# A second attention layer and the choice of experts, per token tile between the slots of one gather

## The reference

```
for i in (0, 1):
    h = x * scale + shift                                   # from c, per layer and half
    f = short_conv_mixer(h) if i == 0 else diff_attention(h)
    x = layer_norm(a * x + gate * f)
    h = x * scale + shift
    x = layer_norm(a * x + gate * peer_ffn(h))

diff_attention: q, k, v = split(h @ w_qkv)                  # 8 heads, 2 scores each, causal
    p = softmax(q k^T / 8 - slope * distance);  a = p[0] - lam * p[1]
    out = rms_norm(a v) * (1 - lambda_init) @ w_o
peer_ffn: q = h @ w_q                                       # 8 heads x 2 x 128
    s = q . sub_keys (2 x 128 scores a head); top 16 of each half; top 16 of the 256 sums
    out = sum over 8 x 16 experts of softmax(top) * gelu(h . u[idx]) * v[idx]
```

## Time and profile before

| | |
|---|---|
| time, median of 3 runs | 2627.26 us (2626.95, 2627.26, 2642.89) |
| the profiled execution | 2643.78 us, span 2641.8 us, mean granted TensorE clock 0.925 |
| busy: PE, PEld, DVE, ACT, POOL | 2226.3, 1465.6, 1677.9, 1113.8, 649.1 us |
| gather, `arena<-experts` | 512 indirect DMAs; its queue moved 587.24 MB |
| weights, `wring<-w_stream` | 284 DMAs of 512 KB |
| chain that ended last | PE 46%, DMA 34%, DVE 10%, ACT 5% of the span |

### The profile page before, as it was taken

One profiled execution on the slowest core, in us unless ns is written; L12 is line 12 of the kernel. 1 busy time (PEld: TensorE's weight loads), 2 busy tenths in 40 slices (PEclk: granted clock), 3 DMA queues, 4 the chain that ended last, 5 costly groups with the idle time before them and its releaser, 6 DMA issues.

```text
span 2641.8 us, 30239 instructions
## 1 busy us (share of the span) xinstructions
PE 2226.3 (84%) x10668; PEld 1465.6 (55%) x10668; DVE 1677.9 (64%) x3715; ACT 1113.8 (42%) x2737; POOL 649.1 (25%) x636
## 2 busy tenths in 40 slices
PE   7678999999999998887787877789688887787786
PEld 7546999876999997522222222277683222222222
DVE  4774667554676666577676666456665766666655
ACT  4343543532453433444444444345344444444443
POOL 0000000000001003444444444300054444344341
PEclk8768999985899988999999999987899999999999
DMA  5223577532557644899999999933258999999995
GB/s 202 78 88 125 172 246 246 184 136 80 179 187 286 236 150 152 315 421 422 421 421 421 421 422 419 401 92 105 66 207 353 421 422 421 422 421 421 422 421 220
DMA packets 130924, 742.66 MB, mean 281 GB/s; under 512 B 14432, under 2 KB 16224, under 8 KB 64992
## 3 DMA queue, kind: packets, MB, share of 16 engines
q0 software_dynamic: 87552, 587.24, 54.5%
q1 hardware_dynamic: 42512, 152.12, 17.5%
q10 hardware_dynamic: 720, 1.51, 0.2%
HBM read 739.76 MB, written 1.05 MB: 280 GB/s over the span
## 4 chain that ended last, share of the span: by engine, by line
PE 46%; DMA 34%; DVE 10%; ACT 5%; issue 3%; POOL 2%; SPq 0%; DVEq 0%; POOLq 0%; ACTq 0%
DMA arena<-experts,arena 34%; PE bank L471 10%; PE bank L473 10%; PE bank L472 10%; PE bank L830 7%; DVE arena L1831 3%; PE bank L586 2%; POOL arena L437 1%; ACT arena L1243 1%; PE bank L573 1%; PE bank L615 1%; ACT arena L1242 1%; PE bank L552 1%; ACT whi L1003 1%; POOL wlo L424 1%
## 5 line engine op out<-in xcount | busy, mean ns | idle before, releaser
L830 PE MATMUL bank<-arena 128*128 128x512 f32 x2048 | 1015.3, 628 | 265.2 <-ACT arena L1243 265.1
L1831 DVE CUSTOM_DVE_ANT_0 arena<-arena 128x1024 f32<-128x1024 f32 x512 | 627.0, 1225 | 444.9 <-DMA arena<-experts,arena 444.7
L830 PEld LDWEIGHTS bank<-arena 128*128 128x128 f32 x2048 | 364.2, 194 | 909.5 <-ACT arena L1243 609.1
L437 POOL DMA_INDIRECT arena<-experts,arena x512 | 541.0, 1057 | 757.5 <-PE bank L830 704.9
L471 PE MATMUL bank<-hTh,whi 128*128 128x256 f32 (+1 forms) x1472 | 439.2, 298 | 52.7 <-DVE hTl L1412 42.6
L1403 DVE TENSOR_TENSOR wlo<-wring,whi 128x1024 fp32r<-128x1024 f32 x260 | 316.4, 1224 | 244.5 <-ACT whi L1003 243.8
L472 PE MATMUL bank<-hTl,whi 128*128 128x256 f32 (+1 forms) x1472 | 430.5, 292 | 0.0
L473 PE MATMUL bank<-hTh,wlo 128*128 128x256 f32 (+1 forms) x1472 | 430.1, 292 | 0.0
L1003 ACT CAST whi<-wring 128x1024 fp32r<-128x1024 f32 x284 | 295.9, 1047 | 239.7 <-PE bank L473 238.3
L1239 ACT ACTIVATE arena<-arena 128x1 f32<-128x1 f32 x512 | 103.6, 202 | 673.4 <-DVE arena L1831 672.5
L471 PEld LDWEIGHTS bank<-hTh,whi 128*128 128x128 f32 x1472 | 291.3, 198 | 66.7 <-issue 51.3
(11 more groups left out here) (253 smaller groups left out, 2473.2 us busy)
## 6 DMA issues: line engine op xcount, KB each, us to landing
wring<-w_stream SPq DMA_DIRECT2D x284, 512.0 KB, 3.6
alibi<-ada_w POOLq DMA_DIRECT2D x64, 512.0 KB, 4.9
arena<-ada_w POOLq DMA_DIRECT2D x32, 512.0 KB, 4.7
arena<-experts,arena POOLq DMA_INDIRECT x512, 15.3
xT<-xT_in SPq DMA_DIRECT2D x1, 1088.0 KB, 5.1
alibi<-alibi_in ACTq DMA_DIRECT2D x1, 1024.0 KB, 6.0
outT<-xT SPq DMA_DIRECT2D x1, 1024.0 KB, 4.6
tab<-tab_in SPq DMA_DIRECT2D x1, 831.0 KB, 6.6
```

The lines of the kernel that those rows point to most:

```text
L437: pool.indirect_dma_start(g_ring[:, r], None, experts[layer], bass.IndirectOffsetOnAxis(idx[:, s // SLOTS, s % SLOTS:s % SLOTS + 1], 0)).t ...
L830: last = mm(banks[2 * t + b][:, :], diag[:, r], g_ring[:, r, D + b * TILE_N:D + (b + 1) * TILE_N], start=s % SLOTS == 0, stop=s % SLOTS == ...
L1831: v.tensor_tensor_reduce(g_ring[:, r, 0:D], g_ring[:, r, 0:D], hrow[:, t], 1.0, 0.0, ALU.mult, ALU.add, act8[:, r:r + 1]).then_inc(dot_don ...
```

## The change

There is one gather of 512 slots: `layer` disappears from the slots, and slot 256 follows slot 255. What stood between the layers is cut into parts, generators that `yield` after each, and run per token tile, beside the slots of the phase that follows (a phase is 128 slots): `mixer_parts(0)` in slots 128 to 255, with the first token tile, whose 128 slots of layer 0 are then summed; `mixer_parts(1)` in slots 256 to 383, which are layer 1's first tile; `last_parts(0)` in 384 to 511; `last_parts(1)` after them. A mixer has 56 parts, due at an even rate from slot 3 of the phase to about slot 94 (`parts_due`). VectorE and ScalarE run a part ahead of the slot it is due at, TensorE three slots earlier (`PE_AHEAD`).

The products of these parts are plain float32 (`half_tile`): tokens are stationary, 128 x 128, and 512 columns of the weight tile move, four products a part and eight a tile, with no splits on ScalarE, VectorE or POOL. Each of the twelve weight tiles is read once for each token tile (`BESIDE`), so 332 quarter tiles are loaded in place of 284. Results come out with tokens on partitions, are copied to rows by ScalarE (`copy_row`) and, for q, k and the experts' queries, turned by TensorE (`turn_row`) and copied again (`copy_turned`). Normalizations are per tile (`norm_parts`): whole blocks 128 x 1024 on VectorE and ScalarE, scale and shift of the next modulation folded in (`both_g`, `both_b`); the root's table is no longer loaded ahead. The lambda of the attention is computed beside slots 40 to 56 of layer 0. The output is written in two halves, the first during the last phase.

```diff
-STEPS = 2 * PEER_HEADS
+TURNS = 4 * PEER_HEADS
+N_SLOTS = 4 * SLOTS
+PARTS_MIXER, PARTS_LAST = 56, 6
+PE_AHEAD = 3
+def parts_due(s):
+    n = (0, PARTS_MIXER, PARTS_MIXER, PARTS_LAST)[s // SLOTS]
+    return max(0, min(n, (s % SLOTS - 3) * n // 92 + 1))
+def parts_begun(s):
+    return parts_due(s) - (parts_due(s - 1) if s % SLOTS else 0)
...
-            for g in range(N_TILES):
+            for g in range(N_LOADS):
                 for c in range(CPT):
                     if g >= 2:
                         sp.wait_ge(lin_done, CPT * (g - 2) + CHUNK_FREE.get(g - 2, (1, 2, 3, 4))[c])
-                    sp.dma_start(wring[:, g % 2, c], w_stream[g, c]).then_inc(w_landed[g % 2][c], 16)
+                    sp.dma_start(wring[:, g % 2, c], w_stream[g if g < N_TILES else g - BESIDE, c]).then_inc(w_landed[g % 2][c], 16)
                 if g == 2:
                     sp.dma_start(wf[:, :, :], wf_in).then_inc(wf_landed, 16)
-            sp.wait_ge(ln_done, 4 * KC)
-            sp.dma_start(out, x2).then_inc(out_done, 16)
-            sp.wait_ge(out_done, 16)
+            for t in range(2):
+                sp.wait_ge(ln2_done, 5 + t)
+                sp.dma_start(out[:, :, t * P:(t + 1) * P], x2[:, :, t * P:(t + 1) * P]).then_inc(out_done, 16)
+            sp.wait_ge(out_done, 32)
...
+            def slot(s):
+                t, r = s // SLOTS % 2, s % RING
+                pe.wait_ge(diag_ready, s + 1)
+                if s % SLOTS == 0 and s >= 2 * SLOTS:
+                    pe.wait_ge(sc_copied, 8 * (s // SLOTS))
+                for b in range(2):
+                    last = mm(banks[2 * t + b][:, :], diag[:, r], g_ring[:, r, D + b * TILE_N:D + (b + 1) * TILE_N],
+                              start=s % SLOTS == 0, stop=s % SLOTS == SLOTS - 1)
+                last.then_inc(slot_used[r], 1)
...
+            def norm_parts(q):
+                pe.wait_ge(f_copied, 2 * q + 2)
+                turn_8(4, lambda c: frow[:, c * P:(c + 1) * P], ft_done)
+                yield
+                yield
+                pe.wait_ge(res2_done, q + 1)
+                for kc in range(KC):
+                    last = mm(banks[6][:, 0:P], table("ones_mean"), xnt[:, kc], start=kc == 0, stop=kc == KC - 1)
+                last.then_inc(mean2_done, 1)
+                yield
+                pe.wait_ge(sq3_done, q + 1)
+                for kc in range(KC):
+                    last = mm(banks[7][:, 0:P], table("ones_mean"), sqt[:, kc], start=kc == 0, stop=kc == KC - 1)
+                last.then_inc(var2_done, 1)
+                yield
+                yield
+            def half_tile(g, half, dst, lhs):
+                if half == 0:
+                    for c in range(CPT):
+                        pe.wait_ge(w_landed[g % 2][c], 16 * (g // 2 + 1))
+                for kc in range(4 * half, 4 * half + 4):
+                    last = mm(dst, lhs[:, kc], wring[:, g % 2, :, kc], start=kc == 0, stop=kc == KC - 1)
+                if half:
+                    last.then_inc(lin_done, CPT)
+            def turn_row(n, x):
+                pe.wait_ge(row_copied, n)
+                k = row_turns[n]
+                if k >= 2:
+                    pe.wait_ge(turn_copied, k - 1)
+                for c in range(CPT):
+                    last = nc.tensor.transpose(banks[4 + x % 2][:, c * P:(c + 1) * P], qrow[x % 2][:, c * P:(c + 1) * P], ident)
...
+            def mixer_parts(t):
+                g0 = G_QKV + BESIDE * t
+                yield
+                yield from norm_parts(2 * t)
+                pe.wait_ge(mod2_ready, 2 * t + 1)
+                for x in range(6):
+                    if 1 <= x <= 4:
+                        turn_row(10 * t + x, x - 1)
+                    if x >= 2:
+                        pe.wait_ge(row_copied, 10 * t + x - 1)
+                    half_tile(g0 + x, 0, banks[6 + x % 2][:, :], hfT)
+                    yield
+                    half_tile(g0 + x, 1, banks[6 + x % 2][:, :], hfT)
+                    yield
+                w = (t + 1) * P
+                pe.wait_ge(turn_copied, 8 * t + 4)
+                pe.wait_ge(row_copied, 10 * t + 6)
+                for h in range(A_HEADS + 3):
+                    if h < A_HEADS:
+                        for p in range(2):
+                            k = 2 * (A_HEADS * t + h) + p
+                            if h:
+                                pe.wait_ge(d_smd, k - 1)
+                            g = slice(64 * p, 64 * p + 64)
+                            mm(banks[4 + p][:, 0:w], dq[g, h], dk[g, h, 0:w], start=True, stop=True).then_inc(d_s, 1)
+                    if 2 <= h < A_HEADS + 2:
+                        n = A_HEADS * t + h - 2
+                        pe.wait_ge(d_ad, n + 1)
+                        if h >= 4:
+                            pe.wait_ge(d_ptc, n - 1)
+                        for kt in range(t + 1):
+                            last = nc.tensor.transpose(banks[6 + n % 2][:, kt * P:(kt + 1) * P],
+                                                       d_a[:, n % 2, kt * P:(kt + 1) * P], ident)
+                        last.then_inc(d_ptd, 1)
+                    if h >= 3:
+                        n, x = A_HEADS * t + h - 3, h - 3
+                        pe.wait_ge(d_ptc, n + 1)
+                        for kt in range(t + 1):
+                            last = mm(banks[2 * t + x // 4][:, (x % 4) * P:(x % 4 + 1) * P], d_at[n % 2][:, kt * P:(kt + 1) * P],
+                                      dv[:, kt, x * P:(x + 1) * P], start=kt == 0, stop=kt == t)
+                        last.then_inc(d_pvd, 1)
+                    yield
+                yield
+                yield
+                yield
+                pe.wait_ge(d_on, t + 1)
+                turn_8(4, lambda c: d_o2[:, c * P:(c + 1) * P], o_turned)
+                yield
+                pe.wait_ge(o_copied, 2 * t + 2)
+                for x in range(2):
+                    for half in range(2):
+                        half_tile(g0 + 6 + x, half, banks[2 * t + x][:, :], oT)
+                        yield
+                yield from norm_parts(2 * t + 1)
+                pe.wait_ge(mod2_ready, 2 * t + 2)
+                turn_8(2 * t, lambda c: hfT[:, c], hrow_done)
+                yield
+                def subkeys(x):
+                    pe.wait_ge(turn_copied, 8 * t + 4 + x + 1)
+                    if x < 2:
+                        pe.wait_ge(hrow_copied, 4 + 2 * t + 2)
+                    else:
+                        pe.wait_ge(sc_copied, 8 + 8 * t + 2 * (x - 1))
+                    for c in range(CPT):
+                        last = mm(banks[2 * t + x % 2][:, c * P:(c + 1) * P], pqt[:, x % 2, c], skT[:, c % 2], start=True, stop=True)
+                    last.then_inc(sk2_done, 1)
+                for x in range(4):
+                    if x == 1:
+                        pe.wait_ge(sk_landed, 32)
+                    if x:
+                        subkeys(x - 1)
+                    if x >= 2:
+                        pe.wait_ge(row_copied, 10 * t + 6 + x - 1)
+                    half_tile(g0 + 8 + x, 0, banks[6 + x % 2][:, :], hfT)
+                    yield
+                    half_tile(g0 + 8 + x, 1, banks[6 + x % 2][:, :], hfT)
+                    yield
+                    turn_row(10 * t + 6 + x + 1, x)
+                    yield
+                subkeys(3)
+                yield
...
+            beside = [None, mixer_parts(0), mixer_parts(1), last_parts(0)]
+            for s in range(early, N_SLOTS):
+                ahead = s + PE_AHEAD
+                for _ in range(parts_begun(ahead) if early + PE_AHEAD <= ahead < N_SLOTS else 0):
+                    next(beside[ahead // SLOTS])
+                slot(s)
+            for _ in last_parts(1):
+                pass
...
+                w = (t + 1) * P
+                for h in range(A_HEADS + 3):
+                    if h < A_HEADS:
+                        for p in range(2):
+                            k = 2 * (A_HEADS * t + h) + p
+                            act.wait_ge(d_nm, k + 1)
+                            if h >= 2:
+                                act.wait_ge(d_ad, A_HEADS * t + h - 1)
+                            af(d_sm[:, k % 4, 0:w], d_sm[:, k % 4, 0:w], ACT.Exp, bias=d_nmx[:, k:k + 1],
+                               accum_out=d_sum[:, k:k + 1]).then_inc(d_exp, 1)
+                    if 2 <= h < A_HEADS + 2:
+                        n = A_HEADS * t + h - 2
+                        act.wait_ge(d_ptd, n + 1)
+                        if h >= 4:
+                            act.wait_ge(d_pvd, n - 1)
+                        nc.scalar.copy(d_at[n % 2][:, 0:w], banks[6 + n % 2][:, 0:w]).then_inc(d_ptc, 1)
+                    yield
...
+            for s in range(early, N_SLOTS):
+                for _ in range(parts_begun(s)):
+                    next(beside[s // SLOTS])
+                gelu(s)
...
+                w = (t + 1) * P
+                for h in range(A_HEADS + 3):
```

(89 more changed lines are left out.)

703 lines of the change are left out of this document (317 added, 386 removed).

## The result

The changed kernel takes 2517.7 us (median of four runs, 2513.2 to 2522.2), the one before 2635.1 in its four (2627.0 to 2649.5): a ratio of 0.955, interval 0.950 to 0.960. Forecast were 2524 us and a range of 2485 to 2592. The profiled execution took 2517.8 us, span 2516.0, against 2643.8 and 2641.8.

What follows compares the result with a forecast made beforehand. The DMA engines, full in both gather plateaus, were taken as the bound. Removing the 248.9 us valley and adding 118 + 10 + 17 = 145 saves 103.9: 2539.9 profiled, 2524 us as median at the lower level, range 2485 to 2592.

Steps and rivals of the forecast that it cites:

- The valley, 248.9 us: Between the two gathers' plateaus the DMA is little used; the change removes all 248.9 us of it.
- Weights, +118: 22 weight tiles fall on full DMA engines during the gather, at 5.4 us each: +118 (110 to 139).
- The row that held both queues: Stretch 1045 to 1075 us with weights and gathers together, giving 5.4 us for a weight tile.
- TensorE, +10: In the query, key, value and experts' queries stages TensorE and DMA loads are even and overlap imperfectly: +10 (0 to 27).
- ScalarE in the heads, +17: Table loads and exponentials in 16 attention heads exceed the DMA's pace by 30 us; ring slack covers 12.6, leaving +17.
- The sum: 118 + 10 + 17 = 145 us replace 248.9, so 103.9 less.
- the lower level of the three runs: Starting level: the profile stands 16.5 us above the runs' median of 2627.3, and the forecast took the lower level.
- DMA alone: Rival: all but the weights vanishes in the ring, 145 shrinks to 118 or 110, 2496 to 2488 us; chance 0.13.
- The clock: Rival: TensorE's clock drops while waiting between small products, at a mean 0.80 giving 2619 us, no change; chance 0.07.
- idle time around loads: Rival: each of 32 table loads in the heads costs ScalarE its length again, 41 us more, 2565; chance 0.05.
- a cost of 3.4 us of slack: In the heads, TensorE's earlier place uses up to 1.36 slots, 3.4 us, of the ring's 9.7 us slack.
- The signs named: Profile signs if right: no valley, given slot paces by stage, two table loads a head, TensorE over 90% busy mid-gather.

Runs made afterwards that it cites:

- experiment 1: Changed kernel with the gather's weight tiles loaded as one eighth of their bytes: 1072.3 us from slot 128 to 511, against 1096.7.
- 3: Changed kernel with two of four products left out of every half tile, all weights loaded: 1088.5 us from slot 128 to 511, against 1096.7.
- Experiment 4: Changed kernel with weights at one eighth of the bytes and half of the products: 1005.6 us from slot 128 to 511, against 1096.7.
- Experiment 12: Changed kernel with TensorE two slots early, not three, and one DMA for a mixer's weight tile: 2509.3 us, ratio 0.951 to the kernel before.

## Why the prediction was right, point by point

- **The valley, 248.9 us.** Right: no slice under 375 GB/s is left in it.
- **Weights, +118.** Measured 22 x 5.26 = 116. The row that held both queues was the one to take. The landing times in the first mixer's phase are 12.3 us for a slot and 10.9 for a quarter tile, and TensorE waited for `wring` twice in the two phases, 2.3 us in all. But 116 is what the weights occupy, not what leaving them out would give: taking some 96 away gave 24.4 (experiment 1).
- **TensorE, +10.** The sum for a phase was good: 123 + 228 = 351 us forecast, 350.4 and 349.1 busy. The two stages took 77.8 and 71.3 us where the forecast had 82 and 71 for the DMA and 80 and 70 for TensorE; the agreement is partly chance, for TensorE was busy only 74.4 and 65.8 in them, and 8.39 and 6.12 MB of weights moved, four and three tiles, not six and four. The warning of two even loads was right, but +10 on top of the DMA was a guess at their coupling, and it hid the main finding: neither load alone decides (experiments 1, 3, 4).
- **ScalarE in the heads, +17.** Wrong: 2. The failing step is the pace that ScalarE was held against, 4.13 us for a part, 1.643 slots at 2.515. It is the pace of slots without weights, yet two weight tiles, 10.5 us, pass in the heads' 18 slots (DMA share 1.01), so a slot takes 3.1 us there and ScalarE's 44.2 busy us fit into 55.7. The sum added two loads that lie in the same slots, of which only the longer counts. Experiment 4 fits this: with thin weights the heads' slots still take 9.4 and 10.9 us more than the plain pace, 20 in all, near the forecast's 17. ScalarE's work was also a little smaller: 44.2 us in the first tile's 18 slots and 47.4 in the second's, where 8 x 5.7 + 3 x 1.5 = 50 were assumed. The 16 heads made 14 loads of the exponential's table, not 16, since a gate's exponential just before shares one; with the loads back to the Gelu's table there were 28 where 32 were forecast. The Trainium skill's drain behind each load (ScalarE: Activation LUTs, What ACT_TABLE_LOAD costs) is not in this trace either: the load's 1.28 us agrees, and 0.02 us separate it from its neighbours.
- **The sum.** 145 forecast; 1096.7 - 383 x 2.515 = 133.5 measured. 116 of it are what the weights occupy and 17.5 the rest, where the forecast had 27. Against the profiled execution of before, the forecast was 2539.9 and 2517.8 came: of these 22.1 us, 11.5 are this and 9.3 the part ahead of slot 0, which varies. The forecast then took 16.5 us off, betting on the lower level of the three runs (2627.3); with a fourth run that median is 2635.1. From there 103.9 less would have been 2531.2. So it is partly luck that 2524 missed by only 6: between the medians the saving was 117.4, not 103.9, 13.5 more, and the starting level was taken 7.8 too low.
- **The rivals.** DMA alone would give 1077 to 1079 for the stretch; the changed kernel is 18 to 19 above it. Experiment 12 ends at 1077.9, but its tiles cost less, 5.0 (15.6% of 382.2 us for twelve), so DMA alone would be 963.2 + 22 x 5.0 = 1073 for it: 5 above. The clock stayed at 0.96 to 0.98 in the two mixers' phases, against 0.86 in the valley. There was no idle time around loads. The side I did not forecast is a lead that is too short: in the text TensorE's three slots appear only as a cost of 3.4 us of slack, while leaving them out costs 181 us.
- **The signs named.** Slots came at 2.5 us in the first and fourth phase, 3.9 in the stage of query, key and value (4.2 forecast), 3.6 in the experts' queries as forecast, 3.1 and 3.3 in the heads (3.6 forecast). TensorE was busy 90% in the mixers' phases, where over 90% was forecast. The tail from the last slot's end to the end took 23.1 us, for 24.1 before.

## What to carry to other kernels

Before work is moved under a stream that is bound by the DMA, add it up against every engine, stage by stage, and in each stage take the highest load and not the sum: here the weights and ScalarE's excess lay in the same slots, and only one of them counted. The second-highest load decides what further savings are worth: of two even loads a large saving on one gave a quarter or a tenth of itself, a small one on the higher came through whole. When engines run interleaved lists in order, give the producer a lead of a few units and measure both sides of it: too little puts the consumer's other work behind the wait (181 us), too much holds back what the producer frees (42 us). Compare such variants over a stretch of the trace that starts behind the untouched part.

## What the runs showed of the hardware that I had not expected

- Weight tiles in rows of 4 KB took 5.26 us of the 16 engines beside a saturated gather, in rows of 16 KB 5.03. The same bytes of the gather in the plateau before cost 5.04 (101.1% of 400 us for 168.22 MB). Longer rows and fewer, larger DMAs came together, so which of them did it stays open. The Trainium skill, DMA: Bandwidth & Descriptors, Rules for kernel authors, advises 1 MiB or more for a DMA; the runs fit that, by 4%, but do not separate it from the rows' length.
- TensorE that was busy 95 to 96% of a stage with plain float32 products ran at a granted clock of 0.98 and 1.00 (query, key and value, in the two mixers' phases); the valley's 0.86 came at 81% busy, with less work, not more.
- A full DMA hides what an engine gains: without the exponentials 18 slots were issued in 49.8 us in place of 55.7, while the DMA moved 419 and 415 GB/s, and the gain was gone some slots later.
